# Roots of the latents and of the key units kept in two rows and spread by products with rows of the identity

## The reference

```
zp = z @ w_in                       # split: c_q (384), c_kv (256), k_pe (64), q_s, k_s, v_s, gate
q  = rms_norm(c_q,  g_q_lat)  @ w_uq    # the "latents": root over 384 and over 256 channels
kv = rms_norm(c_kv, g_kv_lat) @ w_ukv
k  = apply_rope(rms_norm(k_s, g_kn))    # two key heads of 128 channels ("sk")
rms_norm(x, g) = x * rsqrt(mean(x * x) + eps) * g
```

## Time and profile before

| | us |
|---|---|
| median of 3 runs (lowest to highest) | 1592.88 (1592.61 to 1593.03) |
| profiled execution, its own time | 1594.28 |
| its span | 1592.5 |
| PE busy | 1571.4 (99%) |
| DVE busy | 1115.4 (70%) |
| ACT busy | 892.0 (56%) |
| POOL busy | 51.5 (3%) |

### The profile page before, as it was taken

One profiled execution on the slowest core, in us unless ns is written; L12 is line 12 of the kernel. 1 busy time (PEld: TensorE's weight loads), 2 busy tenths in 40 slices (PEclk: granted clock), 3 DMA queues, 4 the chain that ended last, 5 costly groups with the idle time before them and its releaser, 6 DMA issues.

```text
span 1592.5 us, 32062 instructions
## 1 busy us (share of the span) xinstructions
PE 1571.4 (99%) x12402; PEld 1521.8 (96%) x12402; DVE 1115.4 (70%) x1715; ACT 892.0 (56%) x1401; POOL 51.5 (3%) x69
## 2 busy tenths in 40 slices
PE   8999999999999999999999999999999999999998
PEld 8888889999889999999999999999999999999997
DVE  6765676668778665687778665675667777775665
ACT  6655565487784444485546444464445755464443
POOL 0000000000001000003000000000000120000000
PEclk9999999999999999999999999999999999999999
DMA  6552224555444656555455656556554644656553
GB/s 217 147 157 94 72 75 148 171 173 175 141 160 144 202 182 196 180 165 158 135 190 168 199 183 194 178 182 195 177 183 158 198 145 140 200 178 192 181 182 118
DMA packets 74785, 264.03 MB, mean 166 GB/s; under 512 B 8592, under 2 KB 10512, under 8 KB 74704
## 3 DMA queue, kind: packets, MB, share of 16 engines
q1 hardware_dynamic: 69120, 246.76, 49.3%
q0 software_dynamic: 3824, 14.05, 2.7%
q10 hardware_dynamic: 1760, 2.09, 0.5%
HBM read 259.73 MB, written 1.05 MB: 164 GB/s over the span
## 4 chain that ended last, share of the span: by engine, by line
PE 93%; DVE 4%; ACT 2%; DMA 1%; issue 1%; ACTq 0%; SPq 0%; DVEq 0%
PE PS L1662 26%; PE PS L1664 26%; PE PS L1663 26%; PE PS L1927 3%; PE PS L2038 2%; PE PS L1871 1%; PE PS L1939 1%; DVE w_lo L1065 1%; PE PS L1861 1%; PE PS L1847 1%; PE PS L1850 1%; PE PS L1848 1%; ACT w_hi L563 0%; PE PS L2031 0%; PE PS L2030 0%
## 5 line engine op out<-in xcount | busy, mean ns | idle before, releaser
L1662 PE MATMUL PS<-YH,w_hi 128*128 128x256 f32 (+1 forms) x2748 | 789.1, 287 | 3.0 <-ACT work L765 1.6
L1664 PE MATMUL PS<-YH,w_lo 128*128 128x256 f32 (+1 forms) x2748 | 777.0, 283 | 0.0
L1663 PE MATMUL PS<-YL,w_hi 128*128 128x256 f32 (+1 forms) x2748 | 776.4, 283 | 0.0
L1065 DVE TENSOR_TENSOR w_lo<-raw,w_hi 128x1024 fp32r<-128x1024 f32 x465 | 570.4, 1230 | 121.4 <-ACT w_hi L563 118.0
L563 ACT ACTIVATE w_hi<-raw 128x1024 fp32r<-128x1024 f32 x465 | 488.8, 1053 | 112.8 <-DMA raw<-stream 44.6
L1662 PEld LDWEIGHTS PS<-YH,w_hi 128*128 128x128 f32 x2748 | 518.8, 189 | 9.9 <-issue 4.2
L1663 PEld LDWEIGHTS PS<-YL,w_hi 128*128 128x128 f32 x2748 | 517.9, 188 | 2.0 <-issue 0.5
L1664 PEld LDWEIGHTS PS<-YH,w_lo 128*128 128x128 f32 x2748 | 519.6, 189 | 0.0
L1663 PE MATMUL PS<-hL,w_hi 128*128 128x256 f32 x832 | 233.1, 280 | 0.0
L1664 PE MATMUL PS<-hH,w_lo 128*128 128x256 f32 x832 | 233.0, 280 | 0.0
L1662 PE MATMUL PS<-hH,w_hi 128*128 128x256 f32 x832 | 232.6, 280 | 0.0
(11 more groups left out here) (311 smaller groups left out, 1393.3 us busy)
## 6 DMA issues: line engine op xcount, KB each, us to landing
raw<-stream SPq DMA_DIRECT2D x465, 512.0 KB, 4.2
work<-stream POOLq DMA_DIRECT2D x24, 512.0 KB, 4.6
work<-work ACTq DMA_DIRECT2D x10, 136.0 KB, 3.6
X<-x SPq DMA_DIRECT2D x4, 272.0 KB, 4.6
out<-zf SPq DMA_DIRECT2D x8, 128.0 KB, 2.0
work<-work ACTq DMA_DIRECT2D x20, 34.0 KB, 2.7
work<-rope SPq DMA_DIRECT2D x1, 544.0 KB, 7.9
work<-levels POOLq DMA_DIRECT2D x1, 512.0 KB, 4.1
```

Source lines behind the costliest of these rows:

```text
L1065: dve.tensor_tensor(w_lo[:, s.slot, :], raw[:, s.slot % RAW, :], f32(w_hi[:, s.slot, :]), ALU.subtract).then_inc(lo_ready, 1)
L1662: pe.matmul(to, wh, xh, start=start, stop=False, skip_group_check=True)
L1663: pe.matmul(to, wh, xl, start=False, stop=False, skip_group_check=True)
L1664: return pe.matmul(to, wl, xh, start=False, stop=stop, skip_group_check=True)
```

## The change

The roots are kept once, in two rows, in place of 128 equal ones.

- Latents: the matrix of ones gives way to `mean`, two columns for each norm (1/384 in the first, or 1/256 in the second), so that the sums of both norms come out as two rows of bank 0. DVE adds the floor (2x272), ACT takes the root, DVE makes the reciprocal of 2x272. PE now waits for this reciprocal (`cinv_ready`) between slabs 6 and 7, and spreads each row over 128 partitions by a product with a broadcast column of the identity. DVE does the lower part of slab 11 between the reciprocal and the scalings, waits for the spread, and scales the five tiles with the spread rows read from PSUM.
- "sk": the sums come out as two rows by `pick`. ACT takes the root straight from them. DVE makes the reciprocal of 2x272 where it finished the unit. A new unit "sb" at slab 10 holds PE's two spread products, which wait for it (`sinv_ready`), and DVE's multiplication out of PSUM.
- POOL has three more memsets, for `mean`, and one more wait ahead of the last constant.

```diff
-        UR = zf[:, 6:8, :]
+        SROOT, CROOT = RT[0:2, 0, :], RT[0:2, 1, :]
-        UNITS = [("pe", 0), ("sk", 0), ("sq", 0), ("ks", 0), ...
+        UNITS = [("pe", 0), ("sk", 0), ("sb", 0), ("sq", 0), ("ks", 0), ...
-        UNIT_AT = (7, 9, 11, 13, 14, ...
+        UNIT_AT = (7, 9, 10, 11, 13, 14, ...
@@ POOL
-            pool.wait_ge(zeroed, 6)
+            pool.memset(mean[:], 0.0).then_inc(zeroed, 1)
+            pool.wait_ge(zeroed, 7)
+            pool.memset(mean[:, 0, 0:1], 1.0 / 384).then_inc(zeroed, 1)
+            pool.memset(mean[:, 1, 1:2], 1.0 / 256).then_inc(zeroed, 1)
+            pool.wait_ge(zeroed, 9)
             pool.memset(fixed[:, 0:1], EPS).then_inc(consts, 1)
@@ ACT
-                    act.wait_ge(ums_ready, 1)
-                    act.activation(UR, RT[:], ACT.Sqrt).then_inc(uroot_ready, 1)
+                    act.wait_ge(uss_done, sums_before(i + 1))
+                    act.activation(SROOT, PS[0:2, 2, 0:T1], ACT.Sqrt, bias=eps_col[0:2], scale=1.0 / 128).then_inc(uroot_ready, 1)
-                act.activation(RT[:], RT[:], ACT.Sqrt).then_inc(croot_ready, 1)
+                act.activation(CROOT, CROOT, ACT.Sqrt).then_inc(croot_ready, 1)
@@ DVE
-                    step.step(dve.reciprocal(RT[:], RT[:]))
+                    dve.reciprocal(CROOT, CROOT).then_inc(cinv_ready, 1)
+                    split(even(E_KS + 1 + LEAD))
+                    dve.wait_ge(cspread_done, 1)
                     for c in range(5):
-                        dve.scalar_tensor_tensor(cf[:, c, :], cf[:, c, :], C[:, C_CN + c:C_CN + c + 1], RT[:, c // 3, :],
+                        dve.scalar_tensor_tensor(cf[:, c, :], cf[:, c, :], C[:, C_CN + c:C_CN + c + 1], PS[:, c // 3, 0:T1],
-                    if kind == "sk":
-                        dve.wait_ge(uss_done, sums_before(i + 1))
-                        dve.wait_ge(cf_ready, 5)
-                        dve.tensor_scalar(RT[:], PS[:, 2:4, 0:T1], 1.0 / 128, EPS, ALU.mult, ALU.add).then_inc(ums_ready, 1)
+                    if kind == "sk":
+                        dve.wait_ge(uroot_ready, 1)
+                        dve.reciprocal(SROOT, SROOT).then_inc(sinv_ready, 1)
+                        step.wait()
+                        step.up(dve.tensor_tensor(ROT[v], ROT[v], XG[:, v], ALU.add))
+                        return
+                    if kind == "sb":
+                        step.wait()
+                        dve.wait_ge(uss_done, sums_before(i + 1))
+                        last = dve.tensor_tensor(KS[:], ROT[turn(i - 1)], PS[:, 2:4, 0:T1], ALU.mult)
-                for part_of, width in ((0, 384), (1, 256)):
-                    dve.wait_ge(css_done, part_of + 1)
-                    last = dve.scalar_tensor_tensor(RT[:, part_of, :], PS[:, part_of, 0:T1], 1.0 / width, floor_[:], ALU.mult, ALU.add)
-                last.then_inc(cms_ready, 1)
+                dve.wait_ge(css_done, 1)
+                dve.tensor_tensor(CROOT, PS[0:2, 0, 0:T1], floor_[0:2, :], ALU.add).then_inc(cms_ready, 1)
@@ PE
-                    last = pe.matmul(PS[:, c // 3, 0:T1], ones[:], csq[:, c, :], start=(c in (0, 3)), stop=(c in (2, 4)))
+                    last = pe.matmul(PS[0:2, 0, 0:T1], mean[:, c // 3, :], csq[:, c, :], start=(c == 0), stop=(c == 4))
-                            last = pe.matmul(PS[:, 2 + a, 0:T1], ones[:], usq[v][:, a, :], start=True, stop=True)
+                            last = pe.matmul(PS[0:2, 2, 0:T1], pick[:, NH - 1 - a:NH + 1 - a], usq[v][:, a, :], start=a == 0, stop=a == 1)
+                    elif kind == "sb":
+                        pe.wait_ge(sinv_ready, 1)
+                        for a in range(2):
+                            last = pe.matmul(PS[:, 2 + a, 0:T1], ident[0:2, a:a + 1].to_broadcast([2, P]), SROOT, start=True, stop=True)
+                        last.then_inc(uss_done, 1)
                     if i == 0:
-                        pe.wait_ge(croot_ready, 1)
+                        pe.wait_ge(ident_loaded, 16)
+                        pe.wait_ge(cinv_ready, 1)
+                        for a in range(2):
+                            last = pe.matmul(PS[:, a, 0:T1], ident[0:2, a:a + 1].to_broadcast([2, P]), CROOT, start=True, stop=True)
+                        last.then_inc(cspread_done, 1)
```

More of the change, by code:

```diff
@@ L336, in program @@
         usq_ready, uss_done, ums_ready, uroot_ready, uout_ready = sem("usq_ready"), sem("uss_done"), sem("ums_ready"), sem("uroot_ready"), sem("uout_ready")
-        rhi_ready, rlo_ready, cms_ready, us_read, kroot_ready, kinv_ready, xg_ready, qms_ready, qroot_ready = sem("rhi_ready"), sem("rlo_ready"), sem("cms_ready"), sem("us_read"), sem("kroot_ready"), sem("kinv_ready"), sem("xg_ready"), sem("qms_ready"), sem("qroot_ready")
+        rhi_ready, rlo_ready, cms_ready, us_read, cinv_ready, cspread_done, sinv_ready, kroot_ready, kinv_ready, xg_ready, qms_ready, qroot_ready = sem("rhi_ready"), sem("rlo_ready"), sem("cms_ready"), sem("us_read"), sem("cinv_ready"), sem("cspread_done"), sem("sinv_ready"), sem("kroot_ready"), sem("kinv_ready"), sem("xg_ready"), sem("qms_ready"), sem("qroot_ready")
         swapped = [sem(f"swapped{b}") for b in range(2)]
@@ L436, in swaps_up_to @@
         def swaps_up_to(i):
-            return sum({"ks": 0, "kb": 0, "pe": 4, "mq": 4, "sk": 2, "sq": 2}[kind]
+            return sum({"ks": 0, "kb": 0, "sb": 0, "pe": 4, "mq": 4, "sk": 2, "sq": 2}[kind]
                        for k, (kind, _) in enumerate(UNITS[:i + 1]) if turn(k) == turn(i))
@@ L784, in unit_squares @@
                     act.activation(usq[v][:, 2, :], QR[:, j, :], ACT.Square).then_inc(usq_ready, 1)
-                    act.wait_ge(uout_ready, outs_before(older[0] + 1))
+                    act.wait_ge(uout_ready, outs_with(older[0]))
                     act.activation(XG[:, v, 0, :], QR[:, j, :], ACT.Copy, scale=C[:, C_QR:C_QR + 1]).then_inc(xg_ready, 1)
-                elif kind != "kb":
+                elif kind not in ("kb", "sb"):
                     act.wait_ge(job_out, J_KS + 2 if kind == "sk" else J_QS[2 * j + 1] + 1)
@@ L1396, in unit @@
                     v = turn(i)
[L1397 to L1401 removed]
+                    if kind in QUERIES:
                         dve.wait_ge(uss_done, sums_before(i + 1))
@@ L1423, in finish @@
                         return
-                    if kind == "kb":
+                    if kind == "sk":
[8 more added lines that the diff above has]
+                        last = dve.tensor_tensor(KS[:], ROT[turn(i - 1)], PS[:, 2:4, 0:T1], ALU.mult)
+                    elif kind == "kb":
                         step.wait()
@@ L1437, in finish @@
                             last = dve.tensor_tensor(PER[:] if kind == "pe" else QR[:, j, :], ROT[v][:, 0, :], XG[:, v, 0, :], ALU.add)
-                        elif kind == "sq":
+                        else:
                             last = dve.tensor_tensor(QS[:, pair, :], ROT[v], XG[:, v], ALU.add)
-                        else:
-                            step.step(dve.tensor_tensor(ROT[v], ROT[v], XG[:, v], ALU.add))
-                            last = dve.tensor_tensor(KS[:], ROT[v], UR, ALU.mult)
                     last.then_inc(uout_ready, 1)
@@ L1467, in even_layer @@
                     finish_at(p)
-                    split(even(p + LEAD))
+                    if p > E_KS + 1:
+                        split(even(p + LEAD))
                     if i is not None:
```

19 lines of the change are left out of this document (9 added, 10 removed).

## The result

The changed kernel takes 1603.6 us (median of 6 runs, 1599.88 to 1605.58) against 1592.74 for the kernel before (6 runs, 1591.96 to 1593.03): ratio 1.0069, interval 1.0056 to 1.0082, 10.9 us slower. The forecast was 1599.0 with a range up to 1601.4: the direction came out, the size lies outside the range. The profiled execution of after took 1605.58 (span 1603.7), the slowest of the six, so its terms come out somewhat larger than the median's.

What follows compares the result with a forecast made beforehand. TensorE's instruction stream plus its holes bounds the kernel. Holes 3.3 + 2.8, spreads 2.2, less vanished holes 3.1 and old clock loss 1.5, plus new clock losses 2.6: +6.3 us, forecast 1599.0, range 1595.4 to 1601.4.

Steps and rivals of the forecast that it cites:

- first hole: PE between slabs 6 and 7 waits for the latents' reciprocal (cinv_ready): 3.3 us, 3.1 to 3.5.
- second hole: PE before slab 11 waits for the key unit's reciprocal (sinv_ready): 2.8 us, 2.1 to 3.6.
- the overlap: On PE, the 0.16 us by which a product's recorded 0.29 overlaps its successor, added to each hole's idle.
- vanished holes: PE's old holes at 48.12, 56.19 and 60.64 go as DVE and ACT are relieved: 3.1 us back.
- fall of before: PE's old slow clock at slab 13, behind the holes at 60.64 and 62.23, goes: 1.5 us back.
- falls of after: PE's clock falls at each of the two new holes: 1.3 us each, bounds 0 and 2.0, together 2.6.
- sums with two columns: PE's sums with two output columns stream the same 272 columns: no cost, bounds -0.1 to +0.1.
- The bound, and that nothing absorbs: PE is 93% of the chain; behind 66 us a change to its arrival at 66.93 passes fully to the total.
- rival A: Both new PE holes come, but the clock falls at one or none: 1596.6 to 1597.9 us; chance 25%.
- rival B: Swap lands before it matters, no PE hole before slab 11, clock falls once: +2.2, 1595.1 us; chance 10%.
- rival C: A swap issue holds ACT longer, or a slow clock lasts two stretches: +8 to +9, 1601.5 us; chance 5%.
- rival D: Reciprocal ready when slab 6 ends, PE never waits for the small roots: -2.4, 1590.5 us; chance 4%.

Runs made afterwards that it cites:

- experiment 4: Changed kernel with each spread one slab later on PE: 1592.59 us; also with DVE's reciprocal and scalings ahead of its lower-half splits: 1591.97; kernel before 1592.93.
- experiment 2: Changed kernel with the reciprocal of the latents' roots moved ahead of DVE's lower half of slab 10: 1602.72 us (1.006 of the kernel before).
- experiment 6: Kernel before and changed kernel, both unchanged, profiled again: before 1592.87 us twice, changed 1603.37 us.
- Experiments 1 to 3: Changed kernel with unread products in both holes (1598.83 us), first (1600.96), second (1601.27); with reciprocal earlier (1602.72); with latents' part only (1596.76), key unit's only (1599.52).

## Why the prediction was wrong, step by step

The forecast's sum stands here beside one against the two executions near their medians, after at 1603.37 and the first of before at 1592.87, over the stretch from PE's first product to the sums behind slab 13 (12.81 to 75.58 = 62.77, and 12.67 to 65.41 = 52.74: +10.0).

| term | forecast | measured |
|---|---|---|
| first hole | +3.3 | +2.9 (from slab 6 to what follows 6.44, 3.57 before; the idle is 3.15, and 0.18 was there) |
| second hole | +2.8 | +2.7 (2.50 and the overlap) |
| spreads | +2.2 | +2.2 (1.11 each) |
| vanished holes | -3.1 | -2.6 (0.76, 0.84, 0.55 and the overlaps) |
| fall of before | -1.5 | 0 |
| falls of after | +2.6 | +4.6 (1.6 behind the first, 3.0 behind the second) |
| sums with two columns | 0 | +0.5 (the latents' 0.3, the key unit's 0.2) |
| sum | +6.3 | +10.3, of 10.0 |

The overlap is the 0.16 of the prediction. The 1.6 is about 16 products at 0.226 instead of 0.126 apart. The 3.0 is slab 11 with 62.59 to 67.67 = 5.08 instead of 3.03, and its spread with 2.11 instead of 1.11. The rest of the difference of the spans (10.5) lies before and behind the stretch, and I can't place it.

- **The bound, and that nothing absorbs.** Right: 62.40 of 63.00 busy behind the place. That an idle of DVE or ACT pays only through a hole of PE is borne out by experiment 4.
- **First wait, second wait.** Right in place, releaser, chain and size (3.3 and 2.8 against 3.13 and 2.56). The forecast built the second one onto PE's arrival, by way of ACT's copy of slab 7, and in the changed kernel ACT does wait for PE there (5.28 us). The forecast lacks that this holds only while PE is late: in experiment 2 the end of the second wait belongs to the chain behind ACT's swap issues, so that a first hole shortened by 2.06 is worth nothing.
- **Relief and vanished holes.** Right in kind. 0.5 too much was credited, since the 0.98 of the earlier trace rows is 0.55 in the execution nearer to the median. That PE's later holes shrink is also named among the signs of being wrong, which contradicts this term; it is no such sign.
- **The step that failed: the clock.** "A fall cost 1.5 before; part of the slow stretch will lie inside the hole, so 1.3 each, bounds 0 and 2.0." In both profiles of the changed kernel all but at most 0.3 us of a slow stretch lies behind the hole, where PE has work for it. It is also mostly longer than the 3.4 us of the one priced at 1.5: 6.8 and 6.8 us in one profile, 3.4 and 6.8 in the other. Counted on the timelines they cost 2.9 and 3.1, and 1.6 and 3.0. By filling the holes it is 4.9 on the medians where 2.6 was forecast, some 2.4 each: 2.3 of the 4.6 that were missing on the median (10.9 against 6.3). That average lies above the upper bound of 2.0; by the times alone that isn't clear of their intervals, by the three counts of 2.9 to 3.1 it is. One fall of 1.5 was the only row for the price; an upper bound needed the case that the stretch is twice as long. The assumption that part of it falls into the hole came true only in experiment 2, behind 4.77 us of idle, and didn't make it cheaper (3.4).
- **The other half of that step: the fall given back.** 1.5 was subtracted as if each execution of before had that fall. The sum was made against the profiled execution, 1594.28, and then carried over to the median, 1.4 lower, as though the same gain were to be had there. The profile's excess over its median was a hint that the fall was this excess. By experiment 6 an execution at the median loses 0 to 0.3 us to a fall. That is up to 1.5 more of the missing 4.6.
- **Sums with two columns.** Costed at 0 with bounds of 0.1, measured 0.5. With 2.3 and 1.5 that makes 4.3 of the missing 4.6; the holes themselves and what they give back were each 0.5 smaller than forecast, which cancels, and 0.3 is left, unplaced.
- **The clock falling at one or none** (rival A) is refuted for these two holes: each of the two profiles has both falls. Experiments 1 to 3 have five more holes of 2.8 to 4.8 us, and each has its fall. The Trainium skill (TensorE: Matmul & The Clock Gate, "HAM oscillation — how this bites in real kernels"), by which the falls would have stayed away, is not borne out here: they come behind idles of 3.1 and 2.5 us, and once behind 0.85.
- **The swap in time** (rival B) did not happen: it landed 3.8 us behind its issue. The estimate of 2.3 from the Trainium skill (DMA: Bandwidth & Descriptors, "Anatomy of one DMA — SWDGE (gpsimd) path") is too short by 1.5 for it; that section fits another path, GpSimd's, and this swap is issued by ACT.
- **Slower still** (rival C, 1601.5) is nearest to what came, with the reason of its second half: a slow clock that lasts twice as long. It had a chance of 5%. The sum's own upper bounds (3.5 + 3.6 for the holes, 2.0 for each fall) give 8.7 and 1601.6, already outside the range that was stated. **Faster** (rival D) fails at the reciprocal, as argued.
- **POOL.** The last memset starts at 3.79 now against 3.56, PE's filler 0.2 later: hidden, since the first product waits for DVE.

Left open: what decides whether the clock falls behind a short idle, since one execution of before falls behind 0.98 and 0.58 us, another behind 0.85 alone, and a third behind none of 0.76, 0.84, 0.55 and 0.58; what decides how long it stays down; and how much of the spread of after's own runs (5.7 us) is the length of its falls. The runs with a mean clock of 0.993 took 1605.1 to 1605.6 and that with 0.996 took 1599.9, which speaks for nearly all of it, but is no experiment.

## What to carry to other kernels

A wait put on a TensorE that is hardly ever idle costs its length and then the slow clock behind it: here some 2.4 us for each of two holes of about 3, beside the hole. Before a part of a sum is carried from the profiled execution to the median, ask whether that part (a fall of the clock above all) is what sets the two apart. And when a chain gets shorter by moving a step to the bound engine, place that engine's wait one piece of work later: the same arithmetic went from 1603.6 to 1592.6 by that alone.

## What the runs showed of the hardware

- The granted clock fell to the lower level at each of the nine idles of 2.5 to 4.8 us that PE has between its slabs in these traces, between 2.8 us ahead of the first product behind it (experiment 2) and 1.3 us after that (experiment 6), and was at 1.00 where unread products filled the same time.
- Short idles decide nothing by their length here: a single one of 1.07 us (experiment 2) and the pair of 0.55 and 0.58 left the clock at 1.00, a single one of 0.85 had a fall 2.2 us behind it in one execution and none in two others.
- A slow stretch lasted about 3.4, 6.8 or 10.2 us. It cost PE 1.5 to 1.6, 2.9 to 3.1 and 3.4 us where PE had work for it (in the last case PE was idle for its first 2.8 us), and a few tenths where it took the place of a hole.
- A reciprocal takes 1.83 us for 2x272, as for 8x272, against 3.55 for 128x544: columns count, rows don't.
- Ten products of f32 with two columns of weights take 2.39 us to the next product, 0.3 more than with 128 columns (2.09), though both stream 272 columns.
- Five scalings of 128x272 with a factor read from PSUM take 2.12 us, with all of it in SBUF 2.16 (line 1391 of the kernel before).
